# A two-layer mLSTM, attention and convolution backbone: the order of work at the opening of attention, and where the modulation products of the second layer are computed

## The reference, cut to what matters

```
for l in range(2):
    mod = silu(c) @ w_mod[l] + b_mod[l]       # 6 x 1024, once for latent, once for context
    h = rmsnorm(x, g1) * (1 + mod[1]) + mod[0]
    p = h @ w_in[l]                           # 3088 columns, split in three groups
    m = mlstm(p)                              # 4 heads of 64: layernorm per head, gated
    d = diff_attention(p)                     # 4 heads, softmax minus lambda * softmax
    v = conv_module(p)                        # depthwise, 31 taps, layernorm, silu
    x = x + mod[2] * (concat(m, d, v) @ w_out[l])
    h = rmsnorm(x, g2) * (1 + mod[4]) + mod[3]
    x = x + mod[5] * ffn(h)                   # l = 0: SwiGLU; l = 1: top 2 of 8 experts
return rmsnorm(x, g_final)                    # latent tokens only
```

## Time and profile before

| | |
|---|---|
| median of 3 runs | 1502.66 us (1500.58 to 1509.72) |
| profiled execution | 1504.74 us, its span 1503.0 us |
| mean granted TensorE clock | 0.967 of full |
| TensorE busy | 1417.0 us (94%) |
| VectorE busy | 999.2 us (66%) |
| ScalarE busy | 654.0 us (44%) |
| GpSimd busy | 263.4 us (18%) |
| stages, from the timeline | layer 0's attention 249 to 348, output 348 to 399, norm 400 to 413, dense FFN to 774, norm to 788, layer 1's projection to 930, attention 930 to 991, output to 1018, norm and router to 1041, experts to 1490 |

### The profile page before, as it was taken

How to read it: one execution, slowest core, us unless ns; L and a number is a source line. 1 busy time by engine, 2 the same in 40 slices (tenths; PEclk the granted TensorE clock), 3 DMA queues, 4 the chain that set the end, 5 groups by cost and what they waited for, 6 DMA issues and landing times.

```text
span 1503.0 us, 20845 instructions
## 1 busy us (share of the span) xinstructions
PE 1417.0 (94%) x7818; PEld 1158.8 (77%) x7818; DVE 999.2 (66%) x1438; ACT 654.0 (44%) x1039; POOL 263.4 (18%) x194
## 2 busy tenths in 40 slices
PE   5999999779999999999999999978999999999996
PEld 3787787447778888888878898577888888888885
DVE  4745765764564444443558696565988988998996
ACT  3443333572320110010025444554777677677675
POOL 1039954700100000000010992000000000000000
PEclk9999998877999999999999999898999999999998
DMA  9344443331232232322323223406979779877950
GB/s 364 142 175 168 169 169 141 112 113 56 85 127 98 88 109 84 112 78 98 119 84 140 85 85 140 169 1 261 420 300 379 283 298 365 298 302 321 344 200 28
DMA packets 30883, 267.09 MB, mean 178 GB/s; under 512 B 3424, under 2 KB 3552, under 8 KB 4960
## 3 DMA queue, kind: packets, MB, share of 16 engines
q1 hardware_dynamic: 30816, 266.15, 46.5%
HBM read 265.09 MB, written 1.05 MB: 177 GB/s over the span
## 4 chain that ended last, share of the span: by engine, by line
PE 82%; DVE 10%; ACT 3%; issue 3%; DMA 2%; DVEq 0%; SPq 0%; ACTq 0%
PE ps L512 39%; PE ps L933 16%; PE ps L953 7%; PE ps L798 4%; PE ps L530 3%; PE ps L670 2%; PE ps L547 2%; DMA sb_arena<-mod 1%; PE ps L725 1%; PE ps L635 1%; PE ps L519 1%; PE ps L706 1%; DVE sb_h_lo L1481 1%; DVE sb_egu_lo L1924 1%; DVE sb_h_hi L1480 1%
## 5 line engine op out<-in xcount | busy, mean ns | idle before, releaser
L512 PE MATMUL ps<-sb_h_hi,sb_w_hi 128*128 128x512 f32 (+1 forms) x640 | 242.0, 378 | 5.4 <-DVE sb_w_lo L1481 3.5
L512 PE MATMUL ps<-sb_h_hi,sb_w_lo 128*128 128x512 f32 (+1 forms) x640 | 239.8, 375 | 0.0
L512 PE MATMUL ps<-sb_h_lo,sb_w_hi 128*128 128x512 f32 (+1 forms) x640 | 239.6, 374 | 0.0
L2083 POOL TENSOR_SCALAR sb_arena<-sb_arena,sb_small 128x512 f32<-128x512 f32 (+1 forms) x82 | 135.1, 1648 | 66.1 <-DVE sb_arena L1606 58.3
L512 PEld LDWEIGHTS ps<-sb_h_hi,sb_w_hi 128*128 128x128 f32 x640 | 121.2, 189 | 29.9 <-DVE sb_w_lo L1481 4.7
L933 PE MATMUL ps<-sb_egu_lo,sb_h_lo 128*128 128x512 f32 (+1 forms) x384 | 144.3, 376 | 0.0
L512 PEld LDWEIGHTS ps<-sb_h_hi,sb_w_lo 128*128 128x128 f32 x640 | 121.2, 189 | 21.6
L512 PEld LDWEIGHTS ps<-sb_h_lo,sb_w_hi 128*128 128x128 f32 x640 | 121.3, 189 | 20.8
L1480 DVE CAST sb_w_hi<-sb_arena 128x2048 fp32r<-128x2048 f32 (+1 forms) x38 | 45.5, 1197 | 134.5 <-PE ps L512 120.1
L1924 DVE TENSOR_TENSOR sb_egu_lo<-sb_arena,sb_con_r 128x1024 fp32r<-128x1024 f32 x98 | 115.2, 1215 | 15.2 <-ACT sb_con_r L1303 15.1
L1935 DVE TENSOR_TENSOR sb_ew_lo<-sb_arena,sb_ew_hi 128x1024 fp32r<-128x1024 f32 x88 | 107.0, 1216 | 11.5 <-ACT sb_ew_hi L1316 11.5
(11 more groups left out here) (328 smaller groups left out, 3072.1 us busy)
## 6 DMA issues: line engine op xcount, KB each, us to landing
sb_arena<-experts SPq DMA_DIRECT2D x90, 1536.0 KB, 8.6
sb_arena<-mod SPq DMA_DIRECT2D x48, 1024.0 KB, 4.9
sb_arena<-in SPq DMA_DIRECT2D x24, 1024.0 KB, 5.8
sb_arena<-gate SPq DMA_DIRECT2D x11, 1024.0 KB, 4.8
sb_arena<-up SPq DMA_DIRECT2D x11, 1024.0 KB, 4.7
sb_arena<-out SPq DMA_DIRECT2D x8, 1024.0 KB, 4.7
sb_arena<-down SPq DMA_DIRECT2D x8, 1024.0 KB, 4.8
sb_arena<-down SPq DMA_DIRECT2D x4, 768.0 KB, 4.1
```

Source lines behind the costliest of these rows:

```text
L512: ins = pe.matmul(o, left[a], right[b], start=(k == first and n == 0), stop=(k == final and n == len(PRODUCTS) - 1))
L2083: g.tensor_scalar(p, u, w[:, j:j + 1], None, ALU.mult)\
```

## The change

1. **Rows ahead of the deviation.** On ScalarE the copies of the opening's filler rows move from `attention` to the head of `memory_deviation`.
2. **First minima earlier.** VectorE takes unit 0's minima behind the last moments, ahead of its wait for the deviation; TensorE issues the scores of unit 1 in the opening, ahead of `memory_turn`.
3. **Gates' product later.** The product with the gates (`memory_gated`) moves into step 1 of the loop, behind the first combination, and in layer 0 the two splits of its results from steps 2 and 3 to steps 8 and 9 (`MEMORY_SPLIT`).
4. **Modulation spread.** Chunks 0 to 7 instead of 0 to 11 stay in layer 0's attention, 16 to 19 instead of 16 to 23 in layer 1's. The three norms behind take four chunks each: 8 to 11, 12 to 15 and, new, 20 to 23. The spins there shrink (12 to 4, 12 to 4, 6 to 1). The order of loads and the stages on VectorE follow: columns 16 to 39 after layer 1's attention, 40 to 47 ahead of the router. SyncE's first load of experts waits for the last chunk as well.

```diff
...
 DVE_TAPS = (16, 24)
+MEMORY_SPLIT = (8, 2)
 OUT_ORDER = (3, 0, 1, 2)
...
 SPIN = {"first": 3, ("squares", 0, 0): 3, ("squares", 0, 1): 2, ("squares", 1, 0): 2, ("squares", 1, 1): 0,
-        ("norm", 0, 0): 5, ("norm", 0, 1): 12, ("norm", 1, 0): 12, ("norm", 1, 1): 6,
+        ("norm", 0, 0): 5, ("norm", 0, 1): 4, ("norm", 1, 0): 4, ("norm", 1, 1): 1,
         ("heads", 0): 0, ("heads", 1): 5, ("scores", 0): 5, ("scores", 1): 0, ("conv", 0): 0, ("conv", 1): 0,
...
 
-MOD_ATTENTION = (range(0, 12), range(16, MOD_CHUNKS))
-MOD_NORM = {(0, 1): range(12, 14), (1, 0): range(14, 16)}
+MOD_ATTENTION = (range(0, 8), range(16, 20))
+MOD_NORM = {(0, 1): range(8, 12), (1, 0): range(12, 16), (1, 1): range(20, MOD_CHUNKS)}
+MOD_ENDS = ((0, FIRST_MOD - 1), (1, FIRST_MOD - 1), (1, 19), (1, MOD_CHUNKS - 1))
+
+MOD_STAGES = {(0, 2 * FIRST_MOD): "modc_first", (0, 48): "modc", (1, 2 * FIRST_MOD): "modc_first", (1, 40): "modc",
+              (1, 48): "modc_gate"}
 
...
                 dense = [(k, 0, i) for i in range(FF // CHUNK) for k in ("gate", "up")]
-                chunks += dense[:1] + [("mod", 1, i) for i in MOD_NORM[0, 1]] + dense[1:]
+                gap = [("mod", 1, i) for i in MOD_NORM[0, 1]]
+                chunks += gap[:2] + dense[:1] + gap[2:] + dense[1:]
                 chunks += [("down", 0, (i, j)) for i in range(D // CHUNK) for j in range(3)]
-        at = chunks.index(("in", 1, IN_ORDER[0])) + 1
-        chunks[at:at] = [("mod", 1, i) for i in MOD_NORM[1, 0]]
+        at, gap = chunks.index(("in", 1, IN_ORDER[0])), [("mod", 1, i) for i in MOD_NORM[1, 0]]
+        chunks[at:at + 1] = gap[:2] + chunks[at:at + 1] + gap[2:]
+        chunks += [("mod", 1, i) for i in MOD_NORM[1, 1]]
         slot_of = {c: n for n, c in enumerate(chunks)}
...
             sp.wait_ge(*act_done.at(("h", 1, 1, KD - 1)))
+            sp.wait_ge(*pe_done.at(("mod", 1, MOD_CHUNKS - 1)))
             for f in range(ET):
...
                 ins.then_inc(*pe_done.tick(("mod", l, i)))
-                if i and (l, i) != (0, FIRST_MOD):
+                if i and (l, i - 1) not in MOD_ENDS:
                     turn_modulation(l, i - 1)
-                if i == MOD_CHUNKS - 1 or (l, i) == (0, FIRST_MOD - 1):
+                if i == MOD_CHUNKS - 1 or (l, i) in MOD_ENDS:
                     turn_modulation(l, i)
...
                 fill(l, 3 - l)
+                scores(1)
                 memory_turn(l)
...
                         conv_variance(l)
-                    if n + 1 < len(units):
+                    if 1 < n + 1 < len(units):
                         scores(n + 1)
...
             def memory_deviation(l):
+                fill(l, 3 - l)
                 f(spare, eps, ACT.Sqrt)
...
 
-                fill(l, 3 - l)
                 for n in range(attention_steps(l)):
...
                 b = par("b_mod", l)[:, first:last].unsqueeze(2).to_broadcast([P, n, 2])
-                settled(v.tensor_tensor(modc[:, l, first:last], ps[:, 7, 2 * first:2 * last].rearrange("p (m s) -> p m s", s=2),
-                                        b, ALU.add), ("modv", l, first))
+                ins = v.tensor_tensor(modc[:, l, first:last], ps[:, 7, 2 * first:2 * last].rearrange("p (m s) -> p m s", s=2),
+                                      b, ALU.add)
+                if first < 40:
+                    settled(ins, ("modv", l, first))
                 for which, g in ((0, "g1"), (1, "g2")):
...
                                                      par(g, l).unsqueeze(2).to_broadcast([P, KD, 2]), ALU.add, ALU.mult)
-                ins.then_inc(*dve_done.tick(("modc", l) if last == 48 else ("modc_first", l)))
+                ins.then_inc(*dve_done.tick((MOD_STAGES[l, last], l)))
 
...
                 memory_moments(l, NH - 1)
+                maxima(l, 0)
                 dve.wait_ge(*act_done.at(("hstd", l)))
...
                         .then_inc(*dve_done.tick(("hn", l, m)))
+
+            def memory_gated(l):
                 lo = low(l)
...
 
+            def maxima(l, n):
+                h, t = n // (NB - low(l) // P), low(l) // P + n % (NB - low(l) // P)
+                nk = CTX if t < 2 else T
+                u = n % 2
+                for c in range(2):
+                    o = full(("s", l, h, t, c))
+                    v.tensor_reduce(rs[:, u, 2 + c:3 + c], o[:, 0:nk], AX_X, ALU.min)\
+                        .then_inc(*dve_done.tick(("smax", l, h, t, c)))
+
             def attention(l):
...
                 units = [(h, t) for h in range(NH) for t in range(lo // P, NB)]
-
-                def maxima(n):
-                    h, t = units[n]
-                    nk = CTX if t < 2 else T
-                    u = n % 2
-                    for c in range(2):
-                        o = full(("s", l, h, t, c))
-                        v.tensor_reduce(rs[:, u, 2 + c:3 + c], o[:, 0:nk], AX_X, ALU.min)\
-                            .then_inc(*dve_done.tick(("smax", l, h, t, c)))
 
...
                 for n in range(steps):
-                    if n < len(units):
-                        maxima(n)
+                    if 0 < n < len(units):
+                        maxima(l, n)
                     if n == CONV_STEP[l]:
...
                         combine(n - 1)
-                    if n in (2, 3):
-                        dve.wait_ge(*dve_drained.at(("hT", l, n - 2)))
-                        split_mix(l, n - 2)
+                    if n == 1:
+                        memory_gated(l)
+                    k = n - MEMORY_SPLIT[l]
+                    if k in (0, 1):
+                        dve.wait_ge(*dve_drained.at(("hT", l, k)))
+                        split_mix(l, k)
                     if steps - 6 < n < steps - 1:
...
                 else:
-                    modulation(1, 2 * FIRST_MOD, 48)
+                    modulation(1, 2 * FIRST_MOD, 40)
                 residual(l, "y", 16, lambda m: ("y", l, m))
...
                     dve.wait_ge(*dve_drained.at(("ffn", KD - 1)))
+            modulation(1, 40, 48)
             router()
```

## The result

The change makes the kernel 1.3% faster: 1484.77 us median of four runs (1483.42 to 1486.48) beside 1503.24 of the kernel before (1500.58 to 1509.72), ratio 0.9874 with a 95% interval of 0.9851 to 0.9896. The forecast said 1486.5, from 1477 to 1500. The profiled execution took 1486.48 us, 1484.7 of it span, where that of before took 1504.74 and 1503.0. These two are compared first. Lines of the new kernel are numbered 8 to 18 higher: L1708 is L1718 now, L1214 is L1223, L1056 is L1065, L530 is L538.

A forecast was written before the change was run, and what follows sets the result against it. TensorE was taken as the bound, busy 94% of the span. Terms -9.6 - 11.5 + 0.5 + 1.5 + 2.7 = -16.4 gave 1488.3 us profiled, 1486.2 against the median, stated as 1486.5; range 1477 to 1500.

The forecast's parts named there:

- the terms for the attentions: The attention stages: layer 0 was forecast at -9.6 us and layer 1 at -11.5 us.
- Layer 0, opening: Start of layer 0's attention: earlier minima and two splits gone give -5.3 us, bounds -7.1 and -2.7.
- Splits at steps 8 and 9: Layer 0's attention: the two splits, moved to these later steps, cost +1 us (0 to +3).
- Layer 0, four products fewer: Steps 11, 13, 15 and 17 of layer 0's attention: dropping their modulation products gives -5.3 us.
- Layer 1: Layer 1's attention: unit 3's minima 8.2 us earlier; with four products fewer, -11.5 us in all, bounds -7 and -14.
- Norm at 400: Norm at 400 us: two more products and a later load of chunk 11 cost +0.5 us (0 to +3).
- Norm at 775: Norm at 775 us: later input weights, delayed residuals and chunk 15's load cost +1.5 us (+0.5 to +5).
- The first rival: TensorE's clock falls in waits for chunks 11 and 15, slowing norms and attentions: +9, 1512 us; chance 0.08.
- Norm at 1019: Last norm: chunk 23's late load and four products delay the first tile, +2.7 us (+1 to +8).
- The rival by which VectorE and ScalarE bound the attention early: Both attentions: units cost 4 instead of 3.3; layer 1 -6, layer 0 -5, norms +5, 1496 us; chance 0.2.
- the one by which the opening doesn't give what it says: Both openings: table load and bank waits eat the gain; layer 0 -1, layer 1 -3, total 1494.5 us; chance 0.1.

The follow-up runs named there:

- experiment 7: The changed kernel with layer 0's two splits of the memory heads back at steps 2 and 3; 1489.71 us, ratio 0.992.
- 3: The changed kernel with four modulation chunks taken from the norms at 400 and 775 back into layer 0's attention; 1480.03 us, ratio 0.9827.
- 6: The changed kernel with 8 and 10 more spin instructions ahead of the products of chunks 11 and 15; 1482.08 us, ratio 0.9859.
- 10: The changed kernel with five spin instructions added at each step from the tenth on of layer 0's attention; 1479.4 us, ratio 0.9844.
- 11: The changed kernel measured again, unchanged, for a second profile; 1486.19 us, ratio 0.9864.
- experiment 1: The kernel before with the opening's edits alone, layer 0's later splits included, modulation chunks as before; 1488.21 us, ratio 0.9881.
- 9: The kernel of 3 with the dummy square root and its table load ahead of the opening's row copies; 1477.97 us, ratio 0.9831.
- 12: The kernel of 9 with five spin instructions added at even steps from 10 on of layer 0's attention; 1478.75 us, ratio 0.9851.
- experiment 2: The kernel before with the modulation spread alone, its ring order and spins included, openings as before; 1506.56 us, ratio 1.0007.
- 4: The changed kernel with chunks 20 to 23 back in layer 1's attention instead of the last norm; 1492.86 us, ratio 0.9912.
- experiment 5: The changed kernel with two modulation chunks taken from the norm at 775 back into layer 0's attention; 1482.73 us, ratio 0.9857.
- 8: The changed kernel with the opening's modulation rows copied behind the heads' square root again; 1485.63 us, ratio 0.9879.

## Why the prediction was right, and where its steps were not

The total was forecast within 2 us, partly by luck: in the sum the terms for the attentions were too small (21.1 for 29.0) and the one for the norm at 775 was far too small (1.5 for 10), and the two errors, 7.9 and 8.6, cancel.

- **Layer 0, opening (-5.3; bounds -7.1, -2.7).** Unit 3's minima come 5.5 earlier against the last memory sum (18.3 us for 23.8), and to unit 8's another 4.4 goes with the splits, the size that the step gave them and that experiment 7 shows by itself: -9.9 together. What failed is the clock in the step. It put the spin and the scores of unit 2 at the low level throughout, so that their minima would come 2.7 earlier; the clock came back at 260.0, and they came 4.4 earlier (14.4 for 18.8). And it charged 1.8 for product 3 at the low level against the splits; product 3 ran at the high level, and the wait wasn't there. In four more profiles of this opening (3, 6, 10 and 11) the transposes too ran at the high level, and unit 3's minima came 8.1 earlier, at 15.6.
- **Splits at steps 8 and 9 (+1; 0 to +3).** From unit 8's minima to unit 10's it is 8.9 us for 6.6: +2.3, 1.6 of it by experiment 7. Held.
- **Layer 0, four products fewer (-5.3).** From unit 10's minima to the output the profile of after is 8.8 shorter (38.9 for 47.7). But with twelve products this part takes 43.0 to 47.9 (before, 1, 3, 9 and 12, mean 45.7), with eight or ten 38.9 to 42.4 (2, 4, 5, 6, 8, 10 and both of after, mean 40.9): -4.8. Experiment 7, also with eight, took 44.7, and with it the mean is 41.3 and the difference -4.4. The step was sized about right, and the two executions compared stand near the two ends of their groups.
- **Layer 1 (-11.5; opening -8.2).** Unit 3's minima came 8.6 earlier (15.3 for 23.9), by the mechanism described: one table load behind the row, the second at once, no wait of TensorE, clock at 1.00. E is -12.7. The halves differ from the step: experiment 1 puts the opening at -6.0 of E, as TensorE with a product in each unit takes part of the lead back, and the products at -6.7 to -8.9 behind it (55.4 to 48.7 and 46.5), not -3.3.
- **Norm at 400 (+0.5; 0 to +3).** From the sum of squares to the first dense product at full pace it is 13.7 us for 13.9, and the dense part behind takes 0.6 more: +0.4. The delay of the gates' residual is not seen, B is -1.0.
- **Norm at 775 (+1.5; +0.5 to +5).** The step that failed. The 1.7 of the two residuals was right (1.45). From the sum of squares to the first dense product it is 15.4 us for 11.8, +3.6. In experiments 7 and 10, with the same work, it is 13.0: there chunk 15 took 4.8 and 4.7 us to land, was awaited for 1.3 and 1.2, and its product ran at the high level. So 1.2 of the 3.6 is four chunks with the load as the step took it, 1.6 is the load of 6.38 us, and 0.9 is the product at the low level (1.93 for 1.07). The splits that were to make good 2.7 made good 1.2 (from the first tile to the first dense product 3.7 us for 4.9). The other 5.1 of D lies behind; the fall of the clock at 871 to 881 is nearly all of it, as experiment 5 has 4.6 from its fall alone. The first rival had put +5 on the clock behind this norm. The size was met, but by luck: directly behind the norm the low level lasted 0.6 us into the dense part, and the 5 came 95 us later, from a fall that the rival doesn't name. Its condition, a wait of about 2.5 us, wasn't what decided either: waits of 1.79 to 1.88 us were followed by the low level (at 390 after, at 775 in 4 and 8, at 870 in seven profiles). Nor were its sums for the attentions right: it had them at the low level, and layer 1's opening ran at 1.00.
- **Norm at 1019 (+2.7; +1 to +8).** The first tile starts 6.4 behind the sum of squares for 4.0: +2.4. The step said that nothing makes it good, but the router's first products, which start 7.5 behind the sum of squares for 4.7, then take 3.57 for 5.58, since in the profile of before they ran in part at the low level. G is +1.0, and -0.1 in the repeat. F is +1.3; its first products ran at the low level. With what the products were worth in layer 1's attention this move pays 6 to 8 us by time, the only part of the spread that pays.

The rival by which VectorE and ScalarE bound the attention early (1496) fell by the time, though experiments 10 and 12 show that they bound layer 0's last steps; the one by which the opening doesn't give what it says (4 in all) fell by experiment 1, by its time and by its profile (13.0). The drain of 1.38 us that the Trainium skill (ScalarE: Activation LUTs, What ACT_TABLE_LOAD costs) adds to a table load isn't in this trace either: the load at 926.10 ends at 927.38 and the next instruction starts at 927.40. The Trainium skill (TensorE: Matmul & The Clock Gate, HAM oscillation) says that work cut up by waits for loads starts slow behind each. The trace after agrees at two places: 1.93 for 1.07 us behind 2.87 at 769, and 1.93 behind 1.87 at 390. Experiment 7 doesn't: its product behind 2.02 us in the same norm at 400 takes 1.07.

## What stays open

Why the clock falls at 870 us isn't settled. TensorE waits there for VectorE for the same time in the kernels after and before:
```profile
870.32 2.68 PE L678 MATMUL ps<-sb_arena 128*128 128x96 f32 x14 [1.87 <-DVE sb_arena L1632]
```
```profile
882.88 1.80 PE L670 MATMUL ps<-sb_arena 128*128 128x96 f32 x14 [1.81 <-DVE sb_arena L1621]
```
It falls in experiments 2, 4, 5, 6, 8 and in both profiles of after, and not before, nor in 1, 3, 7, 9, 10 and 12. The number of products at 775 doesn't decide it (5 has two and falls; 7 and 10 have four and don't), nor does the low clock in the norm (5 and 10). Of the nine profiles with four products in the norm at 400 seven fall, and of the five with two none.

The traces hold one pattern that separates the two groups. In each of them the moments at which the granted clock changes are evenly spaced, to within 0.1 us. Told in parts of that spacing, the wait at 870 starts at 0.49 to 0.66 in the seven profiles that keep the clock, and at 0.85 or at 0.05 to 0.35 in the seven that lose it. The wait in layer 0's opening (2.92 us, in two profiles 2.83) does the same: it starts at 0.65 to 0.69 in the four profiles that keep the clock, and at 0.89 to 0.98 or at 0.20 in the seven that lose it within 1 us of its end. That speaks for the place in time at which a wait happens to lie. It is a pattern found in fourteen profiles and not an experiment: no kernel shifts that stage by a known amount and leaves the rest. So the 7 us that experiments 7 and 10 have over after in D, of which the shorter load is a part, must not be credited to their edits. Why the load of chunk 15 took 4.7 to 6.4 us is open too.

## What to carry to other kernels

Split a change that has two ideas in it and time them apart before you keep both: here one gave nearly all of the 18 us by time, and of the other one part gave 6 to 8 and the rest cost 5 to 7, so that the change without that rest was among the best versions. A gap in which an engine waits is not free room when what is moved there needs a load of its own: ask when its ring slot comes free, when it lands at the latest that the traces show, and at which clock the engine runs after it has waited. And sum the forecast by stages with boundaries that every profile has; only so can one see that a right total was made of two wrong terms.

## What the runs showed of the hardware

TensorE's level after a wait isn't fixed by the wait's length. Layer 0's transposes in the profile of after, and in that of its repeat:
```profile
255.95 0.66 PE L703 MATMUL ps<-sb_con,sb_small 128*128 128x128 f32 x4 [2.92 <-ACT sb_arena L1223]
256.44 0.91 PE L703 MATMUL ps<-sb_con,sb_arena 128*128 128x128 f32 x4
257.15 3.76 PE L527 MATMUL ps<-sb_con 128*128 128x256 f32 x10
```
```profile
258.82 0.66 PE L703 MATMUL ps<-sb_con,sb_small 128*128 128x128 f32 x4 [2.92 <-ACT sb_arena L1223]
259.32 0.62 PE L703 MATMUL ps<-sb_con,sb_arena 128*128 128x128 f32 x4
259.77 2.32 PE L527 MATMUL ps<-sb_con 128*128 128x256 f32 x10
```
The wait is 2.92 us in both, and only in the first did the clock fall, during the second row. A wait of 2.02 us for chunk 11 was followed by the low level in experiment 2 and by the high one in experiment 7. Nor is a load's time fixed: the same 1 MB chunk, issued at the same place, took from 4.73 to 6.38 us to land. Executions of this one kernel lie up to 16 us apart (1473.84 to 1489.86, mean granted clock 0.977 and 0.971), so that one profile can't say which of two kernels within 5 us is faster, while a stage whose clock is alike repeats to 0.1 (C is 374.9 in four profiles and 375.0 in a fifth).
